# Feed-forward second product by seven block products instead of eight, latent tokens only

## What is computed

```python
def _sq_relu_mlp(h, w1, w2):
    return jnp.square(jax.nn.relu(h @ w1)) @ w2        # w1 1024 x 4096, w2 4096 x 1024
...
h_lat = h_lat + g2 * _sq_relu_mlp(_modulate(_rms_norm(h_lat, norm2_g[i]), sh2, sc2), mlp_w1[i], mlp_w2[i])
if not last:
    h_ctx = h_ctx + cg2 * _sq_relu_mlp(..., mlp_w1[i], mlp_w2[i])
```

## Time and profile before

| | us |
|---|---|
| median of three runs | 2651.51 |
| the profiled execution, its time | 2646.01 |
| its span, first to last instruction | 2644.3 |
| mean granted clock of TensorE | 0.972 of full speed |

### The profile page before, as it was taken

One profiled execution on the slowest core, in us unless ns is written; L12 is line 12 of the kernel. 1 busy time (PEld: TensorE's weight loads), 2 busy tenths in 40 slices (PEclk: granted clock), 3 DMA queues, 4 the chain that ended last, 5 costly groups with the idle time before them and its releaser, 6 DMA issues. The chain is left out here.

```text
span 2644.3 us, 33894 instructions
## 1 busy us (share of the span) xinstructions
PE 2446.0 (93%) x12100; PEld 2001.2 (76%) x12100; DVE 1389.7 (53%) x2325; ACT 852.5 (32%) x1472; POOL 537.4 (20%) x335
## 2 busy tenths in 40 slices
PE   4998989999999999999769688887989999999999
PEld 2667857888888888888567576665668888888887
DVE  4546766344443444434677688883273444344344
ACT  4452134121111211112343488882152121212121
POOL 0000031112111121111200256661122222222220
PEclk9998998999999999999989899999989999999999
DMA  6437520101101001010121211102011111111101
...
DMA packets 74683, 171.51 MB, mean 65 GB/s; under 512 B 36992, under 2 KB 47744, under 8 KB 64128
## 3 DMA queue, kind: packets, MB, share of 16 engines
...
...
## 5 line engine op out<-in xcount | busy, mean ns | idle before, releaser
L916 DVE SCALAR_TENSOR_TENSOR ht<-l_yy_ps,mod,ht 128x512 f32<-128x512 f32 (+1 forms) x640 | 445.5, 697 | 310.0 <-PE l_yy_ps L53 309.5
L51 PE MATMUL l_z_ps<-nh,l_w1h 128*128 128x512 f32 (+1 forms) x1280 | 478.1, 374 | 12.1 <-DVE nl L58 11.3
L52 PE MATMUL l_z_ps<-nl,l_w1h 128*128 128x512 f32 (+1 forms) x1280 | 474.5, 371 | 0.0
L53 PE MATMUL l_z_ps<-nh,l_w1l 128*128 128x512 f32 (+1 forms) x1280 | 474.1, 370 | 0.0
L51 PE MATMUL l_yy_ps<-l_ah,l_w2h 128*128 128x512 f32 (+1 forms) x1280 | 471.3, 368 | 2.1 <-DVE l_al L58 2.1
L52 PE MATMUL l_yy_ps<-l_al,l_w2h 128*128 128x512 f32 (+1 forms) x1280 | 471.1, 368 | 0.0
L53 PE MATMUL l_yy_ps<-l_ah,l_w2l 128*128 128x512 f32 (+1 forms) x1280 | 470.9, 368 | 0.0
L897 DVE TENSOR_TENSOR l_sq<-l_rel 128x512 f32<-128x512 f32 x160 | 118.9, 743 | 569.5 <-ACT l_rel L808 569.4
L51 PEld LDWEIGHTS l_z_ps<-nh,l_w1h 128*128 128x128 f32 x1280 | 244.1, 191 | 59.9 <-DVE nl L58 16.1
L53 PEld LDWEIGHTS l_z_ps<-nh,l_w1l 128*128 128x128 f32 x1280 | 244.2, 191 | 40.5
L52 PEld LDWEIGHTS l_z_ps<-nl,l_w1h 128*128 128x128 f32 x1280 | 244.3, 191 | 40.3 <-issue 0.5
...
## 6 DMA issues: line engine op xcount, KB each, us to landing
l_w1f<-w SPq DMA_DIRECT2D x32, 1024.0 KB, 4.7
l_w2f<-w SPq DMA_DIRECT2D x32, 1024.0 KB, 4.9
maw<-ada SPq DMA_DIRECT2D x24, 1024.0 KB, 5.2
aw<-ada POOLq DMA_DIRECT2D x24, 1024.0 KB, 5.0
...
fw<-fnet_w SPq DMA_DIRECT2D x8, 512.0 KB, 5.1
fx<-x SPq DMA_DIRECT2D x8, 512.0 KB, 5.1
...
```

The costliest lines, as they stand in the source:

```text
L51: pe.matmul(out, lh, rh, start=first, stop=False)
L52: pe.matmul(out, lh, rl, start=False, stop=False)
L53: return pe.matmul(out, ll, rh, start=False, stop=last)
L916: dve.scalar_tensor_tensor(out=h, in0=y_ps[u % 4][:, 0:n], scalar=mod[:, layer, G2, m, v:v + 1], in1=h, op0=ALU.mult, op1=ALU.add).then_in ...
```

## The change

Only the second product on latent tokens is done otherwise. Within a pair it is a 2 x 2 block product: `A11`, `A12`, `A21`, `A22` are the blocks of the weights (first index the half of the output features, second the chunk `c`), `B11`, `B21` the squared activations of token block 0 for `c` = 0, 1, and `B12`, `B22` those of block 1. Strassen's identity in Winograd's form makes the four output blocks from seven products. Each product `M1` to `M7` is four groups (one per 128 output features) of three matmuls, and the groups of a product use the four banks in turn. Products are chained in the banks: `M3` adds onto `M5`, `M1` onto `M2`, then `M6`, `M7`, `M4` onto `M1`, and the bank is read after every product. So a pair has 7 x 4 group reads on latent tokens in place of 16. Three reads of four are VectorE's (`acc`, as before), the fourth (`SIDE`, bank 3) is a scaled ScalarE read into a buffer `side`, which GpSimd adds to `ht` (`side_read`, `add`).

Four weight sums (`S1` to `S4`, GpSimd) and four activation differences (`T1` to `T4`, VectorE) are new. Weights of the second product are now split in seven blocks of 512 elements (eight in layer 0, whose context tokens keep the old way with a bank of their own), and those of the first in two halves of 1024, with a load of 512 KB each into a single half-size buffer `w1f`. The high part of the activations is a copy of VectorE's square, no longer a square of its own. There are five operand buffers `ah`/`al`: `B21` takes that of `T1` and waits for `M5`, `T4` that of `B22` and waits for `M3`. The output stores go by 128 x 512 halves.

```diff
+    TOK = {"B11": (0, 0), "B12": (1, 0), "B21": (0, 1), "B22": (1, 1), "C0": (2, 0), "C1": (2, 1)}
+    Z_LOOP = ["B11", "B12", "C0", "B22", "B21", "C1"] if C else ["B11", "B12", "B22", "B21"]
+    Z_FIRST = ["B11", "B21", "B12", "B22"] + (["C0", "C1"] if C else [])
+    HI_LOOP = (["B11", "T1", "C0", "B22", "T2", "T3", "C1", "B21", "T4"] if C else
+               ["B11", "T1", "B22", "T2", "T3", "B21", "T4"])
...
+    SLOT = {"B11": 0, "T1": 0, "T2": 0, "T4": 0, "B12": 1, "T3": 1, "B22": 2, "B21": 3}
...
+    PLACE = {"A11": 0, "S3": 0, "A12": 1, "S4": 1, "A21": 2, "A22": 3, "S1": 4, "S2": 4}
+    RING = {"S1": 0, "S4": 1, "A12": 2, "A11": 3, "S2": 0, "S3": 1, "A22": 2, "A21": 3}
+    W_ORDER = ["S1", "A11", "A12", "S4", "S2", "S3", "A22"] + (["A21"] if C else [])
...
+    MUL = {"M5": ("S1", "T1"), "M3": ("S4", "B22"), "M2": ("A12", "B21"), "M1": ("A11", "B11"), "M6": ("S2", "T2"),
+           "M7": ("S3", "T3"), "M4": ("A22", "T4")}
+    STARTS = ("M5", "M2", "M1")
+    INTO = {"M5": (1, 1), "M3": (0, 1), "M2": (0, 0), "M1": (0, 0), "M6": (0, 1), "M7": (1, 1), "M4": (1, 0)}
+    EARLIER = {"M3": None, "M5": None, "M2": None, "M1": "M2", "M6": "M3", "M7": "M5", "M4": None}
+    ROWS = ["M5", "M3", "M2", "M1", "M6", "M7", "M4"]
...
-                def load1(p, row):
-                    sp.wait_ge(s_w1l, p + PRE)
-                    sp.dma_start(w1f[:], w1[layer, row].rearrange("a p k n -> p (a k) n")).then_inc(s_w1, 16)
+                def load1(p, row, c):
+                    sp.wait_ge(s_w1l, p * 2 + (PRE + c))
+                    sp.dma_start(w1f[:], w1[layer, row, c].rearrange("a p k n -> p (a k) n")).then_inc(s_w1, 16)
 
                 def load2(p, rows):
-                    sp.wait_ge(s_w2l, p + PRE)
-                    sp.dma_start(w2f[:], w2[layer, rows].rearrange("c p n -> p c n")).then_inc(s_w2, 16)
-                load1(0, slice(0, 1))
+                    sp.wait_ge(s_w2l, p * NW + PRE)
+                    for h in range(2):
+                        sp.dma_start(w2f[:, 2 * h:2 * h + 2], w2[layer, rows, :, 512 * h:512 * h + 512].rearrange("c p n -> p c n")).then_inc(s_w2, 16)
...
+                def weights(p):
+                    pool.wait_ge(s_w2, p * 32 + 32)
+                    summed(p, "S1", "A21", ALU.add, "A22")
+                    low2(p, "S1")
+                    pool.wait_ge(s_w2l, p * NW + (PRE + 1))
+                    summed(p, "S2", "S1", ALU.subtract, "A11")
+                    low2(p, "A11")
+                    pool.wait_ge(s_w2l, p * NW + (PRE + 2))
+                    summed(p, "S3", "A11", ALU.subtract, "A21")
+                    low2(p, "A12")
+                    pool.wait_ge(s_w2l, p * NW + (PRE + 3))
+                    summed(p, "S4", "A12", ALU.subtract, "S2")
+                    low2(p, "S4")
+
+                def add(p, prod):
+                    _, h = chunk(prod, SIDE)
+                    i = SIDE_TO[prod, SIDE]
+                    pool.wait_ge(s_ya, p * NS + (PRE + i))
+                    pool.wait_ge(s_add, p * NS + (PRE + i - 1))
+                    pool.tensor_tensor(h, h, side[(i - 1) % 2][:], ALU.add).then_inc(s_add, 1)
...
+                def outputs(p, more):
+                    if more:
+                        low1(p + 1, 1)
+                    low2(p, "S2")
+                    add(p, "M5")
+                    low2(p, "S3")
+                    for prod in ("M3", "M2", "M1"):
+                        add(p, prod)
+                    for name in W_ORDER[6:]:
+                        low2(p, name)
+                    for prod in ("M6", "M7", "M4"):
+                        add(p, prod)
...
-                with pool.Fori(1, PAIRS) as p:
-                    low1(p)
-                    low2(p)
+                            low1(0, 0)
+                        if v == KC:
+                            low1(0, 1)
+                weights(0)
+                low1(1, 0)
+                outputs(0, True)
+                with pool.Fori(1, PAIRS - 1) as p:
+                    weights(p)
+                    low1(p + 1, 0)
+                    outputs(p, True)
...
+                        act.wait_ge(s_sqr, z_at(p, name, zorder))
+                    if name == "B21":
+                        act.wait_ge(s_y, y_at(p, "M5", 3))
...
+                def outputs(p, order, more):
+                    if more:
+                        act.wait_ge(s_z, p * U1 + (PRE + U1))
+                        high1(p + 1, 1)
+                    high(p, "B21", order)
+                    side_read(p, "M5")
+                    high2(p, "S2")
+                    high(p, "T4", order)
+                    side_read(p, "M3")
+                    high2(p, "S3")
+                    side_read(p, "M2")
+                    side_read(p, "M1")
...
+                def pair(p, more=True):
+                    relu(p, "B11", Z_LOOP)
+                    high(p, "B11", Z_LOOP)
+                    for name in ("S1", "A11"):
+                        high2(p, name)
+                    relu(p, "B12", Z_LOOP)
+                    high(p, "T1", Z_LOOP)
+                    for name in ("A12", "S4"):
+                        high2(p, name)
+                    if C:
+                        relu(p, "C0", Z_LOOP)
+                        high(p, "C0", Z_LOOP)
+                    if more:
+                        high1(p + 1, 0)
+                    relu(p, "B22", Z_LOOP)
+                    for name in ("B22", "T2", "T3"):
+                        high(p, name, Z_LOOP)
+                    relu(p, "B21", Z_LOOP)
...
+                    need = {"T1": "B12", "T2": "B22", "T3": "B22", "T4": "B21"}[name]
+                    dve.wait_ge(s_sqr, z_at(p, need, zorder))
+                    if old:
+                        dve.wait_ge(s_al, p * NH + (PRE + horder.index(old) + 1))
...
+                def acc(p, prod, m):
+                    c, h = chunk(prod, m)
+                    dve.wait_ge(s_y, y_at(p, prod, m))
+                    if EARLIER[prod]:
+                        dve.wait_ge(s_acc, p * NA + (PRE + ACC_TO[EARLIER[prod], m]))
+                    dve.scalar_tensor_tensor(out=h, in0=y_ps[m][:], scalar=mod[:, layer, G2, c, 0:1], in1=h,
+                                             op0=ALU.mult, op1=ALU.add).then_inc(s_acc, 1)
...
+                    diff(p, "T3", "B22", "B12", Z_LOOP, HI_LOOP)
+                    for name in ("B22", "T2", "T3"):
+                        low(p, name, HI_LOOP)
+                    square(p, "B21", Z_LOOP)
+                    if C:
+                        square(p, "C1", Z_LOOP)
+                        low(p, "C1", HI_LOOP)
...
+                def outputs(p, zorder, horder, final=False):
+                    dve.wait_ge(s_acc, p * NA + PRE)
+                    for m in range(3):
+                        acc(p, "M5", m)
+                    diff(p, "T4", "B21", "T2", zorder, horder)
+                    acc(p, "M3", 0)
+                    low(p, "B21", horder)
+                    acc(p, "M3", 1)
+                    acc(p, "M3", 2)
+                    acc(p, "M2", 0)
+                    low(p, "T4", horder)
...
-                pair(0, True)
-                with pe.Fori(1, LOOPED) as p:
-                    pair(p, False)
-                if out is not None:
-                    pair(LOOPED, False, True)
-                    pe.wait_ge(s_acc, PAIRS * U2 + PRE)
-                    for t in range(4, QB):
-                        out_tile(t)
+                                s = RING["A%d%d" % (1 + m // 2, c + 1)]
...
-        "w1": a["mlp_w1"].reshape(DEPTH, KC, P, DFF // (2 * P), 2 * P).transpose(0, 3, 2, 1, 4),
+        "w1": a["mlp_w1"].reshape(DEPTH, KC, P, DFF // (2 * P), 2, P).transpose(0, 3, 4, 2, 1, 5),
```

More of the change, by code:

```diff
@@ L727, in mlp @@
         z_ps, y_ps = banks(N + "z_ps", NZ, ph), banks(N + "yy_ps", 4, ph)
         ms_ps = y_ps
[L729 to L733 removed]
+        sq, rel, rb = slot[0:2], slot[2:4], side
+        psq = [w2f[:, i] for i in range(SQ)]
+        OB = 6
@@ L741, in mlp, with evicted @@
+        ON_DVE = [i >= 8 and i % 2 == 1 for i in range(len(HALVES))]
+        DVE_TO = [sum(ON_DVE[:i + 1]) for i in range(len(HALVES))]
+        def evicted(eng, i):
+            if ON_DVE[i]:
+                eng.wait_ge(s_od, DVE_TO[i])
+            else:
+                eng.wait_ge(s_oa, i + 1 - DVE_TO[i])
         with nc.Block() as block:
@@ L836, in _ @@
                 rms(0)
-                high1(0)
+                high1(0, 0)
                 norm(0)
+                high1(0, 1)
                 norm(1)
-                high2(0)
-                for b in range(NB):
-                    hidden(0, 2 * b)
-                    hidden(0, 2 * b + 1)
-                    if b == 0 and NB > 2:
-                        norm(2)
-                with act.Fori(1, LOOPED) as p:
-                    high1(p)
-                    high2(p)
-                    for u in range(U1):
-                        hidden(p, u)
@@ new lines, in _ @@
```

(64 more changed lines are left out.)

427 lines of the change are left out of this document (274 added, 153 removed).

## The result

The changed kernel takes **2719.53 us** (median of four runs, 2715.55 to 2721.47), the kernel before 2652.48 beside it: a ratio of 1.0254, 95% interval 1.0236 to 1.0272. It is slower by 67 us. The forecast said slower by 24 us.

A forecast was written before the change was run, and what follows sets the result against it. TensorE alone was taken to bound the feed-forward part. Terms -87.1 + 54.6 + 23.8 + 25.5 + 7 gave +24 us: 2670 against the profiled 2646.0, 2676 against the median; own range 2660 to 2695, overall 2625 to 2720.

The forecast's parts named there:

- can't work at once: VectorE passes over two SBUF operands and GpSimd passes: five or six such meetings a pair instead of one.
- 0.55 us behind it: A VectorE pass over two SBUF operands that starts under a GpSimd pass ends 0.55 us after that pass.
- Rival 1: The two engines don't hold each other up at passes of 512; -38 us, 2613 us, chance 0.13.
- What was removed: Second product on latent tokens: 84 matmuls instead of 96, 2.72 us a pair, -87.1 us over both layers.
- I take 1.2: Price in us of GpSimd's new 512-element passes, put between 1.04 and 1.25; 2.3 for 1024.
- the walk of layer 1's pair: Step-by-step timing of a layer 1 pair: 3.9 us lost, period 44.7 us, +54.6 us over 14 pairs.
- rival 2: GpSimd passes of 1.04 us, so `B22`'s square precedes the low part of `w1`; 2649 us, chance 0.22.
- M2 1.25 us lost: Layer 1 pair: `M2` waits for the low part of `B21`, costing 1.25 us with the restart.
- rival 3: Worse than walked: GpSimd at 1.25, slower load, no VectorE overlap, or clock drops (+20 us); 2710 us, chance 0.2.
- 1.7 us a pair: Layer 0 loss from `M2`'s late operands and a short first-eviction wait; period 54.1 us, +23.8 us over 14 pairs.
- First pairs: First pair of each layer: +12 us in layer 0 and +13.5 in layer 1 from late operands and loads.
- near 401: Layer 0's first pair: squares and sums ahead of the first hidden matmul end near 401 us instead of 387.04.

The follow-up runs named there:

- run 1: Changed kernel with GpSimd's low parts of the next pair's `w1` behind the additions of `M3` and `M6`, and ScalarE's second-half copy later: 2646.75 us, ratio to before 0.9997.
- Run 6: Changed kernel with `w1` low parts later, Relu of `B22` earlier, squares on ScalarE, layer 0's low part of `B21` ahead of `T4`: 2598.27 us, 0.9811 of before.
- run 9: Changed kernel with 15 extra matmuls of 512 columns on TensorE between `M5` and `M3` in layer 1's 14 looped pairs: 2712.59 us, ratio to before 1.0236.
- run 8: Changed kernel with GpSimd's low part of `w1`'s second half behind the norm's squares in each layer's first pair: 2720.99 us.
- run 10: Run 6 plus, in each layer's first pair, ScalarE's copy of `S4` behind the high part of `B22`: 2595.38 us, ratio to before 0.9782.

## Why the prediction was wrong in size

**The mechanism was right, but counted on one side only.** That two engines "can't work at once" is what costs: run 1 moves two GpSimd passes a pair and takes back all 67 us. GpSimd's passes are held in their turn, which the forecast left out (below). The place was right (the square of `B22` behind the low part of `w1`), and "0.55 us behind it" to the hundredth. The Trainium skill (SBUF — State Buffer, section SBUF: two separate sides) states an exclusive lock held for the full instruction, against VectorE operations with two SBUF inputs. The trace agrees: 2.80 us under a pass of 2.39, 1.15 under passes of 256, 0.745 for evictions, which read PSUM, whatever GpSimd does. Rival 1 (2613 us) needed passes that take turns at no cost, and is excluded.

**What was removed** is right: 84 matmuls, 0.2267 us each. Run 6 earns it but for 0.5 and 0.7 us a pair.

**Step that failed: the price of a GpSimd pass, "I take 1.2", bounds 1.04 to 1.25.** It is 1.29. The error was in "a quarter of the subtraction of 2048 is 1.15 with no fixed part": with the 2.39 us for 1024, each 512 elements cost 1.10 us and each pass 0.19. The pass of 640 at 1.25 us was no bound, being another operation at another pace. The trace of the kernel before had the row that would have given it, an addition of 256 elements in the attention:

```profile
L1377 POOL TENSOR_TENSOR of<-ot 128x256 f32<-128x256 f32 x32 | 23.4, 731 | 125.4 <-ACT ot L1423 125.4
```

From 0.73 us for 256 and 4.61 for 2048, 512 elements come to 0.73 + 3.88 / 7 = 1.28 us. The forecast also misread as "GpSimd's own pace was not hurt there": those squares of 256 took 1.06 us, as long as a square of 512 elsewhere (1.04), so they were held too. In the walk of layer 1's pair seven passes, to the low part of `S4`, lie ahead of the place where `B22` meets `w1`: 0.6 us later by the price, 0.33 more by one of them, the sum `S3`, which is held in its turn (1.62 us, below). GpSimd starts 0.1 late, and the pass of 1024 takes 2.39 us instead of 2.3. The first group of `M3` comes 3.68 us late instead of 2.5. The point of rival 2 ("the square of `B22` must start before GpSimd takes the low part of `w1`") was missed by 0.14 us of 20.

**"M2 1.25 us lost"** was masked in the kernel after, and is 1.22 us when TensorE keeps its clock (run 9).

**The clock** stood in rival 3 and not in the sum. It does drop, in 13 of 14 pairs; the 1.5 us there are right for one drop (1.4), but slow matmuls cover a wait that comes later anyway. Net it is 0.25 x 14 = 3.5 us, not 20.

Together layer 1's loop came to +41 instead of +16: per pair 3.68 + 1.22 for the two waits where 2.5 + 1.25 stood, 0.25 for the clock, and a rest of 0.5 us, restarts and small delays that were not measured singly, where I had 0.15: 5.65 in place of 3.9.

**Layer 0, "1.7 us a pair":** it is 2.8. `M2`'s wait is 1.53 as walked (1.6), but "a short wait for the first eviction", taken as next to nothing, is 0.90 us, and each has its restart. That is 1.07 x 14 = 15 us.

**First pairs:** 11.6 and 13.7 us against 9.3 and 10.8, near enough, but for a wrong reason in layer 0. The late start ("near 401", measured 402.4) costs nothing (run 8); 8.3 us are the same meetings as in the loop (run 1).

**All in all** the table's two sums are 51 us apart: 25 in layer 1's loop (16.5 of them in `M3`'s wait), 15.5 in layer 0's, 6.7 in the line between the layers, 5 in the first pairs, -0.7 at the end. The time came nearest to rival 3 (2710 us). Of the causes that it lists the price went beyond its 1.25, and the clock cost little; the loads of 512 KB landed after 3.4 us (median), and VectorE's neighbours overlap as assumed (two in 1.29 us).

**Left open:** whether the 5.7 us between the layers belong to the change. Also, no run took apart what is left of the first pairs. In run 10 layer 1's still takes 2.0 us more than before, with 12 matmuls less, and its waits ahead of `M5`, `M3` and `M2` are shown but not traced to their causes.
